# Down projection in another order, and its weight sums on VectorE: one core of a decoder layer

## The chip, the cores and the metric

The kernel runs on one NeuronCore of one Trainium2 chip. The metric is the time of one execution in microseconds (us) on the device. The kernel before takes 1776.47 us, the median of three runs.

## The reference

One decoder layer on a sequence of 256 positions, width 2048, all in float32: two parallel branches (a spatial gating unit and a gated delta rule), an output projection, a SwiGLU feed-forward network and a gated embedding. The change lies in the feed-forward network and in what follows it directly:

```python
D_FF = 5632
h = rms_norm(x, norm_ffn[i])
f_gate, f_up = jnp.split(h @ w_gate_up[i], 2, axis=-1)   # w_gate_up: 2048 x 11264
x = x + (jax.nn.silu(f_gate) * f_up) @ w_down[i]         # w_down: 5632 x 2048
ple_gate = jax.nn.sigmoid(rms_norm(x, ple_norm[i]) @ w_ple_gate[i])
```

## The kernel before, in words

**Halves.** All weights come from memory in tiles of 128 x 1024 float32 (512 KB), called halves and numbered in the order in which TensorE uses them. To get float32 accuracy from the faster matmul type, each half is split in two: ScalarE (ACT) rounds it into `whi` (`split_hi`, lines 423 and 433), VectorE (DVE) takes the rest, `wlo` (`split_lo`, line 447). TensorE (PE) multiplies `whi` by both parts of the other operand and `wlo` by its high part. There are four slots for raw weights and four for `whi` and `wlo` (`RING`), and the splits run three halves ahead (`LEAD`): at stage n of a phase ScalarE and VectorE first split half n+3 and then do whatever else the program puts at stage n. The high part of half n+3 can't be made before TensorE has finished half n-1, whose slot it takes. Every engine works its list strictly in order.

**Pairs and forms.** The gate-up and down projections go through "pairs": two blocks of 512 columns computed together, block 0 in the PSUM tile `acc[0]`, block 1 in `acc[1]`. A part of each pair is done by a seven-product scheme of the Strassen kind on 2 x 2 blocks (two tiles of positions, two blocks of columns, two halves of depth): a "unit". A unit reads four halves, B11, B12, B21, B22, into slots of their own (`unit[...]`), forms four sums of weights from them (T3 = B12 + B22, T1 = B12 + B11, T2 = T1 + B22, T4 = B21 + T2) and multiplies the seven matrices B11, T1, B21, B22, T3, T2, T4 with sums of the input (`sx`, made by `sum_inputs` and `sums_low` on VectorE and `sums_high` on ScalarE). T1 takes the slot of B12 and T4 that of B21. A form costs TensorE 6 matmuls of 128 x 512 (lines 1111 and 1114); a plain half costs 12 (lines 475 and 481). The products go to `ps[0]`, `ps[1]`, `acc[0]` (B21 and T4) and `acc[1]` (B22).

**Who makes the sums.** VectorE makes T3 and T2 (`sum_t3`, `sum_t2`, lines 2210 and 2220). T1 and T4 are made by transfers that add: GpSimd waits and issues `dma_start(..., accum_op=ALU.add)` of one SBUF tile onto another (lines 749 and 752), 16 units with two each.

**The order.** `PAIRS` writes the halves of each pair as a string: `f` is the next form of the current unit in the fixed order of `UNIT_FORMS`, `0` and `1` are plain halves of block 0 and block 1. The phases around the change run in this order: `ffn0` (plain), `ffn1` to `ffn5`, `down_a0`, `down_a1` (the down projection of the first 3072 features, two pairs of column blocks), `ffn6` to `ffn10`, `down_b0` and `down_b1` (the rest; `down_b1` is plain). An ffn pair has 19 halves and one unit, `down_a0` and `down_a1` 30 halves and two units each, `down_b0` 26 halves and two units. `SyncE` issues all loads in the order of use, each waiting until its slot is read.

**What happens at the ends of pairs.** When the last B11 of a pair is done, ScalarE copies `ps[0][:, 0]` (`copy_p1`); when T2 and T3 are done, VectorE combines `ps` (`lower_sums`, `upper_sums`, lines 2273 to 2283). TensorE's first form of the next pair, B11, waits for `upper_sums`, and for `ps_free`, which VectorE sets after `f_low` (lines 2169 and 2171), the low part of the transposed product of the last ffn pair. Its first plain half of block 0 waits for `acc_read[0]`, B22 for `acc_read[1]`. In an ffn pair these are given by `gate_add` (stage 13) and `up_add` (stage 0 of the next pair). In a down pair VectorE adds first the sums (`add_sums`, line 2304) and then the PSUM tile (`add_pair`, which is `add_block`, lines 2142 and 2144) to the residual `xtok`, in that order; line 2144 is the release of `acc_read`. These lie at stages 29 of one down pair and 0 and 1 of what comes next.

Of the kernel before, what the change touches and what calls it, by code (L numbers as in the profile page):

```python
# [23 lines left out]
ALU = mybir.AluOpType  # L24
# [49 lines left out]
UNIT_FORMS = (B11, T1, B21, B22, T3, T2, T4)  # L74
# [34 lines left out]
for _name, _order in PAIRS.items():  # L109
    _counts, PAIR_UNITS[_name] = {"0": 0, "1": 0}, []  # L110
    for _n, _c in enumerate(_order):
        _h = H0[_name] + _n
        if _c == "f":
            if not PLACE or len(PLACE[-1]) == len(UNIT_FORMS):
                PAIR_UNITS[_name].append(len(PLACE))
                PLACE.append({})
            _form = UNIT_FORMS[len(PLACE[-1])]
# [9 lines left out]
U_BASE, _u = {}, 0  # L127
for _name in PAIR_NAMES:
    U_BASE[_name] = _u
    _u += 4 if _name.startswith("ffn") else 6  # L130
# [41 lines left out]
def build(nc, win, wba, wa, wb, wo, wgu, wd, wpg, wpp, xT_d, xk_d, pT_d, cols_d, hv_d, gmw_d, gmb_d, fin_d, out_d):  # L172
# [180 lines left out]
    t1_added, t4_added, t_made, s_summed, s_split = (sem("t1_added"), sem("t4_added"), sem("t_made"), sem("s_summed"), sem("s_split"))  # L353
    p1_copied, u_made, sum_full = sem("p1_copied"), sem("u_made"), sem("sum_full")
# [193 lines left out]
    with nc.Block() as block:  # L548
# [78 lines left out]
        def _(pool):  # L627
# [142 lines left out]
        def _(pe):  # L770
# [366 lines left out]
            def pair(name, after={}, free_from=None):  # L1137

                for n in range(PER[name]):
                    h = H0[name] + n  # L1140
                    if h in PLAIN:
                        block, c = PLAIN[h]
                        if c == 0 and block == 0:
                            acc_free(pe, name, 0, 0, 0)
                        x = unit_of(name, 0)[0]
                        first = c == 0 and (True if block == 0 else (1,))
                        use_half(pe, name, 0, n, block, first, False, 2 * len(PAIR_UNITS[name]) + c, x, rows=True)
                    else:
# [28 lines left out]
            gemm("down_b1", 0, 0, 2 * PART_B, 0, 0, fx, rows=True, after={1: lambda: turn_x(1, 0), 4: lambda: turn_x(1, 1)})  # L1177
# [37 lines left out]
        def _(act):  # L1215
# [436 lines left out]
            def ffn(i, turned, extra={}):  # L1652
# [8 lines left out]
                             21: (copy_p1("down_a0", PART_A),)})  # L1661
            pair("down_a1", {17: (copy_p1("down_a1", PART_A),), 27: (sums_high(3, 0, PLACE[PAIR_UNITS["down_a1"][1]][T2]),)})
# [6 lines left out]
                             19: (copy_p1("down_b0", FB // 2),)})  # L1669
            for n in range(PER["down_b1"]):  # L1670
                split_hi(act, "down_b1", 0, n)
                if n == 2:
                    x_high(1, 0, C_PLE)
                if n == 5:
# [61 lines left out]
        def _(dve):  # L1736
# [486 lines left out]
            for n in range(2 * HWIDE):  # L2223
# [41 lines left out]
            def lower_sums(name, up, turned):  # L2265

                def stage():
# [3 lines left out]
                    dve.wait_ge(u_made, U_BASE[name])  # L2271
# [26 lines left out]

            def add_sums(name, half, sums, b):
# [20 lines left out]
            def ffn(i, before, turned, extra={}):  # L2320

                name, k = f"ffn{i}", PAIR_UNITS[f"ffn{i}"][0]
                stages = {0: before[0], 1: before[1], 11: (lower_sums(name, up_sum[i], i - 1),), 12: (upper_sums(name, up_sum[i]),),
                          13: (gate_add(i),), 14: (sum_t3(k + 1),), 15: (turned_low(i - 1),) if turned else (), 18: (sum_t2(k + 1),)}
# [4 lines left out]
            def finish_f(i):  # L2329
# [9 lines left out]
            pair("down_a0", {0: (up_add(5),), 1: (product(5),), 4: (turned_low(5),), 7: (sum_inputs(fx, 4, 2),), 9: (sums_low(2, 0),),  # L2339
                             11: (sum_t3(k + 1),), 17: (sum_t2(k + 1),), 25: (sum_t3(k + 2),),  # L2340
                             27: (lower_sums("down_a0", down_up, PART_A),), 28: (upper_sums("down_a0", down_up),),
                             29: (add_sums("down_a0", 0, gate_sum, 0), add_pair("down_a0", 0, 0, MB + 1), sum_t2(k + 2))})
            pair("down_a1", {0: (add_sums("down_a0", 1, down_up, 1),), 1: (add_pair("down_a0", 1, 1, MB + 2),),
                             7: (sum_t3(k + 3),), 13: (sum_t2(k + 3),), 21: (sum_t3(k + 4),),
                             25: (lower_sums("down_a1", down_up, PART_A), sum_inputs(ax, 0, 3)), 26: (upper_sums("down_a1", down_up),),
                             27: (add_sums("down_a1", 0, gate_sum, 2), sums_low(3, 0)),
                             28: (add_pair("down_a1", 0, 2, MB + 3), sum_t2(k + 4)), 29: (add_sums("down_a1", 1, down_up, 3),)})
            ffn(6, ((add_pair("down_a1", 1, 3, 2 * MB),), ()), False)
# [5 lines left out]
            pair("down_b0", {0: (up_add(10),), 1: (product(10),), 4: (turned_low(10),), 7: (sum_inputs(fx, 4, 5),), 9: (sums_low(5, 0),),  # L2354
                             10: (sum_t3(k + 1),), 15: (sum_t2(k + 1),),
                             24: (lower_sums("down_b0", down_up, FB // 2), upper_sums("down_b0", down_up)),
                             25: (add_sums("down_b0", 0, gate_sum, 0), add_pair("down_b0", 0, 0, 2 * MB + 1))})
            for n in range(PER["down_b1"]):
                split_lo(dve, "down_b1", 0, n)
                if n == 0:  # L2360
                    add_sums("down_b0", 1, down_up, 1)()
                    add_pair("down_b0", 1, 1, 2 * MB + 2)()
                if n == 2:
                    x_low(1, 0, C_PLE)
                if n == 5:
# [117 lines left out]
```

## Time and profile before

| | us |
|---|---|
| median of 3 runs | 1776.47 (1775.42 to 1777.78) |
| profiled execution | 1779.04 |
| its span | 1777.4 |
| PE busy | 1747.2 (98%) |
| DVE busy | 1268.2 (71%) |
| ACT busy | 922.7 (52%) |
| POOL busy | 256.7 (14%) |
| mean granted TensorE clock | 0.993 of 2.4 GHz |
| `unit<-unit` adding transfers | 32 of 512 KB, 6.2 to landing |

Busy time is the time in which an engine executed something. In a timeline the number before the engine is start and length; in square brackets stands how long the engine had been idle before and what released it. PE matmuls overlap each other a little, so the distance from start to start is the cost of one group, not the printed length.

### The profile page before, as it was taken

What the parts mean: (1) busy time and instruction counts of PE and PEld (TensorE: products, weight loads), DVE (VectorE), ACT (ScalarE), POOL (GpSimd) and SP (SyncE); (2) the same over time, 40 slices, a digit from 0 to 9 for tenths busy, and PEclk for the clock granted to TensorE, in tenths of its full rate; (3) what the DMA queues carried; (4) which work ended last, traced back from release to release, by engine and by line L of the source; (5) the groups of instructions that cost most, each with busy time, mean ns of one, the idle gap of its engine ahead of it and who ended that gap; (6) DMA issues with size and microseconds to landing.
All of it is one profiled execution on the core that took longest, in us unless ns stands there. A gap on an engine that the chain in (4) does not pass through costs nothing.

```text
span 1777.4 us, 24725 instructions
## 1 busy us (share of the span) xinstructions
PE 1747.2 (98%) x8888; PEld 1470.5 (83%) x8888; DVE 1268.2 (71%) x1496; ACT 922.7 (52%) x1019; POOL 256.7 (14%) x379
## 2 busy tenths in 40 slices
PE   9999999999999999999999999999999999998998
PEld 7888888889888888888888888887778888877887
DVE  7698887988867545455566778776777787767666
ACT  7764464555555444444445555545455555544455
POOL 5035070431610000000010000000000000001011
PEclk9999999999999999999999999999999999999999
DMA  8566465474657666666667776776777777755663
GB/s 272 173 187 189 145 204 167 141 218 135 193 167 227 190 194 191 192 189 189 189 196 219 217 225 211 236 212 197 207 223 229 231 215 225 211 163 166 191 210 133
DMA packets 108614, 349.59 MB, mean 197 GB/s; under 512 B 23712, under 2 KB 24112, under 8 KB 108272
## 3 DMA queue, kind: packets, MB, share of 16 engines
q1 hardware_dynamic: 88448, 320.12, 57.1%
q0 software_dynamic: 5696, 22.81, 6.7%
q10 hardware_dynamic: 14384, 5.52, 1.3%
q8 instruction: 54, 0.88, 0.2%
q14 instruction: 32, 0.26, 0.0%
HBM read 328.46 MB, written 3.16 MB: 187 GB/s over the span
## 4 chain that ended last, share of the span: by engine, by line
PE 83%; issue 5%; POOL 4%; DVE 3%; DMA 2%; ACT 2%; ACTq 0%; POOLq 0%; DVEq 0%; SPq 0%
PE acc L475 40%; PE acc L481 20%; PE acc L454 7%; PE acc L459 3%; PE ps L1111 3%; PE acc L1111 2%; POOL blk_t L676 2%; POOL blk_x L678 2%; PE ps L1114 1%; DVE wlo L447 1%; DMA unit<-unit 1%; PE acc L1114 1%; ACT whi L433 1%; PE ps L1085 1%; DMA diagT<-inv_out 0%
## 5 line engine op out<-in xcount | busy, mean ns | idle before, releaser
L447 DVE TENSOR_TENSOR wlo<-raw,whi 128x1024 fp32r<-128x1024 f32 x540 | 682.9, 1271 | 399.0 <-ACT whi L433 386.7
L433 ACT ACTIVATE whi<-raw 128x1024 fp32r<-128x1024 f32 x539 | 568.3, 1058 | 601.5 <-PE acc L481 468.2
L475 PE MATMUL acc<-whi,ax 128*128 128x512 f32 x2176 | 540.7, 390 | 1.6 <-DVEq L2144 1.4
L475 PEld LDWEIGHTS acc<-whi,ax 128*128 128x128 f32 x2176 | 406.2, 188 | 86.7 <-issue 1.8
L481 PE MATMUL acc<-wlo,ax 128*128 128x512 f32 x1088 | 291.1, 389 | 0.0
L481 PEld LDWEIGHTS acc<-wlo,ax 128*128 128x128 f32 x1088 | 204.2, 188 | 42.9 <-DVE wlo L447 0.3
L454 PE MATMUL acc<-ax,whi 128*128 128x512 f32 x896 | 228.6, 397 | 0.1
L454 PEld LDWEIGHTS acc<-ax,whi 128*128 128x128 f32 x896 | 160.9, 189 | 30.4 <-ACTq L1445 0.3
L447 DVE TENSOR_TENSOR wlo<-unit,whi 128x1024 fp32r<-128x1024 f32 x112 | 136.9, 1224 | 63.2 <-ACT whi L423 57.0
L423 ACT ACTIVATE whi<-unit 128x1024 fp32r<-128x1024 f32 x112 | 118.7, 1061 | 103.0 <-PE acc L481 56.5
L475 PE MATMUL acc<-whi,fx 128*128 128x512 f32 x512 | 133.0, 404 | 8.6 <-DVEq L2144 8.6
L459 PEld LDWEIGHTS acc<-ax,wlo 128*128 128x128 f32 x896 | 122.2, 190 | 9.0
L475 PEld LDWEIGHTS acc<-whi,fx 128*128 128x128 f32 x512 | 99.7, 196 | 30.5 <-DVEq L2144 9.4
L459 PE MATMUL acc<-ax,wlo 128*128 128x256 f32 x896 | 124.8, 282 | 0.0
L742 POOL TENSOR_TENSOR sqsum<-sqsum,t 128x512 f32<-128x512 f32 x16 | 27.6, 1725 | 462.4 <-ACT t L1577 461.8
L676 POOL TENSOR_TENSOR blk_t<-blk_m,blk_x 128x60 f32<-128x60 f32 (+24 forms) x124 | 67.4, 543 | 99.8 <-DMA blk_m<-inv_in 90.4
L481 PE MATMUL acc<-wlo,fx 128*128 128x512 f32 x256 | 69.2, 393 | 0.0
L678 POOL TENSOR_TENSOR blk_x<-blk_x,blk_t 128x60 f32<-128x60 f32 (+24 forms) x124 | 64.5, 521 | 9.7
L749 POOL DMA_DIRECT2D unit<-unit x16 | 14.0, 874 | 356.2 <-DVE unit L2210 356.2
L475 PE MATMUL acc<-whi,mx 128*128 128x512 f32 x256 | 63.6, 391 | 0.0
L475 PE MATMUL acc<-whi,yb 128*128 128x512 f32 x256 | 63.2, 389 | 0.0
L481 PEld LDWEIGHTS acc<-wlo,fx 128*128 128x128 f32 x256 | 48.9, 191 | 10.4
(331 smaller groups left out, 1784.4 us busy)
## 6 DMA issues: line engine op xcount, KB each, us to landing
raw<-in_win SPq DMA_DIRECT2D x223, 512.0 KB, 4.2
raw<-in_wgu SPq DMA_DIRECT2D x136, 512.0 KB, 4.4
raw<-in_wd SPq DMA_DIRECT2D x64, 512.0 KB, 4.4
unit<-in_wgu SPq DMA_DIRECT2D x40, 512.0 KB, 4.6
raw<-in_wb SPq DMA_DIRECT2D x32, 512.0 KB, 4.1
raw<-in_wo SPq DMA_DIRECT2D x32, 512.0 KB, 4.0
unit<-unit POOLq DMA_DIRECT2D x32, 512.0 KB, 6.2
raw<-in_wpg SPq DMA_DIRECT2D x32, 512.0 KB, 4.2
```

The source lines that it names most:

```text
L423: nc.scalar.activation(whi[:, s], unit[b][:], ACT.Copy).then_inc(hi_done, 1)
L433: nc.scalar.activation(whi[:, s], raw[:, src], ACT.Copy).then_inc(hi_done, 1)
L447: nc.vector.tensor_tensor(wlo[:, s], src, whi[:, s].bitcast(F32), ALU.subtract).then_inc(lo_done, 1)
L454: return nc.tensor.matmul(o, whi[:, s, kt, m * P:(m + 1) * P], x[:, k].rearrange("p q n -> p (q n)"), start=begin, stop=end, skip_group_ch ...
L459: return nc.tensor.matmul(o[:, 0:SEQ], wlo[:, s, kt, m * P:(m + 1) * P], x[:, k, 0], start=begin, stop=end, skip_group_check=True)
L475: nc.tensor.matmul(into[buf][:, m], x[:, WIDE_K * h + kt, q, m * P:(m + 1) * P], whi_w[:, s, kt], start=(m in first if isinstance(first, t ...
L481: mm = nc.tensor.matmul(into[buf][:, m], x[:, WIDE_K * h + kt, 0, m * P:(m + 1) * P], wlo_w[:, s, kt], start=False, stop=last and kt == WI ...
L676: chain(g.tensor_tensor(tmp, blk_m[:, j + 1:32, j:j + 1].to_broadcast([P, r, c]), blk_x[:, j:j + 1, 0:c].to_broadcast([P, r, c]), ALU.mult ...
L678: chain(g.tensor_tensor(blk_x[:, j + 1:32, 0:c], blk_x[:, j + 1:32, 0:c], tmp, ALU.add), v + 3 + 2 * j)
L742: g.tensor_tensor(sqsum[:], sqsum[:], piece(t[1], a), ALU.add).then_inc(res["added"], 1)
L1111: mm(out, x(q, kt), whi_w[:, s, kt], start=begin and kt == 0 and q == 0, stop=False, skip_group_check=True)
L1114: last = mm(out, x(0, kt), wlo_w[:, s, kt], start=False, stop=end and kt == WIDE_K - 1, skip_group_check=True)
```

## The change

The forms get letters of their own, so that the order string says which form comes where (`a` B11, `b` T1, `c` B21, `d` B22, `e` T3, `g` T2, `h` T4). The ffn pairs keep their order. The second part of each down pair is reordered; in its last unit T4 comes before T2 and T3, and in `down_b0` B21 comes before T1. T1 and T4 are made by VectorE (`sum_t1`, `sum_t4`), and the adding transfers and GpSimd's waits for them are gone. The release of `acc[0]` and `acc[1]` after down pairs becomes a stage of its own (`add_acc`), separate from `add_sums`. `turned_low` moves from stage 4 to stage 3 in `down_a0` and `down_b0`. `copy_p1` and `lower_sums` wait for a count of residual updates (`res["x"]`, `X_DONE`) instead of `u_made`. Two transposes of `down_b1` go one half later.

```diff
-UNIT_FORMS = (B11, T1, B21, B22, T3, T2, T4)
+FORM_OF = {"a": B11, "b": T1, "c": B21, "d": B22, "e": T3, "g": T2, "h": T4}
-FFN_ORDER = "f0f0f0f0f0ff0111111"
+FFN_ORDER = "a0b0c0d0e0gh0111111"
-         "down_a0": "0000f0f0f0f0f1f1f1f1ff1ff1ff11", "down_a1": "f0f0f0f0f0f0f0f0f1f1f1f1f1f111",
+         "down_a0": "0000a0b0c0d0eg1ha1b1cd1hg1e111", "down_a1": "a0b0c0d0e0g0h0a0b1c1d1h1g1e111",
-         "down_b0": "0000f0f0ff1f1f1ff1fff1fff1"}
+         "down_b0": "0000a0c0bd1h1egac1bd1h1ge1"}
...
+X_DONE = {name: MB * (1 + (name != "down_a0" and PAIR_NAMES.index(name) > PART_A - 1)) for name in PAIR_NAMES}
+X_DONE["down_a1"] = MB + 2
...
-            for k in range(N_UNITS):
-                pool.wait_ge(unit_in[B11], 16 * (k + 1))
-                pool.wait_ge(t_made, 2 * k + 1)
-                pool.dma_start(unit[T1][:], unit[B11][:], accum_op=ALU.add).then_inc(t1_added, 16)
-                pool.wait_ge(lo_done, PLACE[k][B21] + 1)
-                pool.wait_ge(t_made, 2 * k + 2)
-                pool.dma_start(unit[T4][:], unit[T2][:], accum_op=ALU.add).then_inc(t4_added, 16)
...
-            gemm("down_b1", 0, 0, 2 * PART_B, 0, 0, fx, rows=True, after={1: lambda: turn_x(1, 0), 4: lambda: turn_x(1, 1)})
+            gemm("down_b1", 0, 0, 2 * PART_B, 0, 0, fx, rows=True, after={2: lambda: turn_x(1, 0), 5: lambda: turn_x(1, 1)})
...
+            def sum_t1(k):
+                def stage():
+                    dve.wait_ge(unit_in[B11], 16 * (k + 1))
+                    dve.wait_ge(t_made, 2 * k + 1)
+                    v.tensor_tensor(unit[T1][:], unit[B12][:], unit[B11][:], ALU.add).then_inc(t1_made, 1)
+            def sum_t4(k):
+                def stage():
+                    dve.wait_ge(lo_done, PLACE[k][B21] + 1)
+                    dve.wait_ge(t_made, 2 * k + 2)
+                    v.tensor_tensor(unit[T4][:], unit[B21][:], unit[T2][:], ALU.add).then_inc(t4_made, 1)
...
+            def add_acc(name, half, b):
+                def stage():
+                    count = 2 * [x for x in PAIR_NAMES if x.startswith("down")].index(name) + half + 1
+                    dve.wait_ge(half_used, pair_end(name, half) + 1)
+                    x = xtok[:, :, WIDE * b:WIDE * (b + 1)]
+                    v.tensor_tensor(x, acc[half][:], x, ALU.add).then_inc(acc_added, 1)
+                    dve.wait_ge(acc_added, count)
+                    dve.sem_inc(acc_read[half], 1)
...
-                    dve.wait_ge(u_made, U_BASE[name] + 4 + half)
+                    dve.wait_ge(u_made, U_BASE[name] + (2, 4)[half])
-                    v.tensor_tensor(x, x, sums, ALU.add).then_inc(u_made, 1)
+                    v.tensor_tensor(x, x, sums, ALU.add).then_inc(res["x"], 1)
...
-          13: (gate_add(i),), 14: (sum_t3(k + 1),), 15: (turned_low(i - 1),) if turned else (), 18: (sum_t2(k + 1),)}
+          13: (gate_add(i),), 14: (sum_t3(k + 1),), 15: (turned_low(i - 1),) if turned else (), 16: (sum_t1(k + 1),), 18: (sum_t2(k + 1),)}
           (and 4: (sum_t4(k),) in the same dictionary)
...
+pair("down_a0", {0: (up_add(5),), 1: (product(5),), 3: (turned_low(5),), 6: (sum_t4(k),), 7: (sum_inputs(fx, 4, 2),), 9: (sums_low(2, 0),),
+                 11: (sum_t3(k + 1), sum_t1(k + 1)), 14: (sum_t2(k + 1),), 18: (sum_t4(k + 1),),
+                 24: (add_acc("down_a0", 0, 0), sum_t3(k + 2)), 26: (sum_t1(k + 2),), 27: (lower_sums("down_a0", down_up, PART_A),),
+                 28: (upper_sums("down_a0", down_up),), 29: (add_sums("down_a0", 0, gate_sum, 0),)})
+pair("down_a1", {0: (add_acc("down_a0", 1, 1),), 1: (sum_t2(k + 2),), 2: (sum_t4(k + 2),), 3: (add_sums("down_a0", 1, down_up, 1),),
+                 7: (sum_t3(k + 3),), 9: (sum_t1(k + 3),), 10: (sum_t2(k + 3),), 12: (sum_inputs(ax, 0, 3),), 17: (sum_t4(k + 3),),
+                 23: (add_acc("down_a1", 0, 2),), 24: (sum_t3(k + 4),), 26: (sum_t1(k + 4),), 27: (lower_sums("down_a1", down_up, PART_A),),
+                 28: (sums_low(3, 0), upper_sums("down_a1", down_up)), 29: (add_sums("down_a1", 0, gate_sum, 2),)})
+ffn(6, ((add_acc("down_a1", 1, 3),), (sum_t2(k + 4),)), False, {3: (add_sums("down_a1", 1, down_up, 3),)})
...
+pair("down_b0", {0: (up_add(10),), 1: (product(10),), 3: (turned_low(10),), 5: (sum_t4(k),), 7: (sum_inputs(fx, 4, 5),), 9: (sums_low(5, 0),),
+                 11: (sum_t3(k + 1), sum_t1(k + 1)), 13: (sum_t2(k + 1),), 16: (sum_t4(k + 1),),
+                 22: (add_acc("down_b0", 0, 0),), 25: (lower_sums("down_b0", down_up, FB // 2),)})
             for n in range(PER["down_b1"]):
                 split_lo(dve, "down_b1", 0, n)
                 if n == 0:
+                    upper_sums("down_b0", down_up)()
+                    add_sums("down_b0", 0, gate_sum, 0)()
+                if n == 1:
+                    add_acc("down_b0", 1, 1)()
                     add_sums("down_b0", 1, down_up, 1)()
```

## Rows read from the trace of the kernel before

**Rows 1.** Timeline of PE, end of `down_b0`, start of `down_b1` (start, us, instruction, count, [idle before]).
```profile
1598.49 1.07 PE L1111 MATMUL ps<-whi,sx 128*128 128x512 f32 x4
...
1603.03 1.07 PE L481 MATMUL acc<-wlo,fx 128*128 128x512 f32 x4
1608.93 3.78 PE L475 MATMUL acc<-whi,fx 128*128 128x512 f32 x8 [4.84 <-DVEq L2144]
...
1614.08 2.00 PE L475 MATMUL acc<-whi,fx 128*128 128x512 f32 x8
```
**Rows 2.** Timeline of PE, first form of `down_a0`.
```profile
1202.12 1.08 PE L481 MATMUL acc<-wlo,fx 128*128 128x512 f32 x4
1206.86 1.38 PE L1111 MATMUL ps<-whi,fx 128*128 128x512 f32 x4 [3.65 <-DVEq L2171]
...
1212.69 1.08 PE L1111 MATMUL ps<-whi,sx 128*128 128x512 f32 x4
```
**Rows 3.** Timeline of PE, first plain half of `down_a1`.
```profile
1261.20 0.61 PE L1114 MATMUL ps<-wlo,fx 128*128 128x512 f32 x2
1265.54 3.63 PE L475 MATMUL acc<-whi,fx 128*128 128x512 f32 x8 [3.72 <-DVEq L2144]
...
1269.98 1.09 PE L1111 MATMUL ps<-whi,sx 128*128 128x512 f32 x4
```
**Rows 4.** Timeline of PE, first plain half of `ffn6`.
```profile
1329.39 0.61 PE L1114 MATMUL ps<-wlo,ax 128*128 128x512 f32 x2
1331.38 2.11 PE L475 MATMUL acc<-whi,ax 128*128 128x512 f32 x8 [1.37 <-DVEq L2144]
...
1335.61 1.98 PE L475 MATMUL acc<-whi,ax 128*128 128x512 f32 x8
```
**Rows 5.** Timeline of PE, first form of `down_b0`.
```profile
1555.51 1.07 PE L481 MATMUL acc<-wlo,fx 128*128 128x512 f32 x4
1560.28 2.04 PE L1111 MATMUL ps<-whi,fx 128*128 128x512 f32 x4 [3.70 <-DVE fx L2169]
...
1567.19 1.09 PE L1111 MATMUL ps<-whi,sx 128*128 128x512 f32 x4
```
**Rows 6.** Windows after the gap in `ffn6`: length, busy of PE, PEld, DVE, ACT, POOL, granted clock, DMA.
```profile
1331.00:1333.00 2.00, 1.62 (x7) 1.37 (x8) 1.76 (x3) 0.16 (x1) 0.00 (x0) 1.00 0.59 231
```
**Rows 7.** Timeline of ACT at the start of `down_a0` and of `down_a1`.
```profile
1200.62 1.01 ACT L1594 ACTIVATE fx<-ps 128x1024 fp32r<-128x1024 f32 x1
...
1260.71 1.06 ACT L423 ACTIVATE whi<-unit 128x1024 fp32r<-128x1024 f32 x1 [4.54 <-DMA unit<-unit]
```
**Rows 8.** Timeline of DVE, end of `ffn5` and start of `down_a0`.
```profile
1187.14 1.23 DVE L447 TENSOR_TENSOR wlo<-raw,whi 128x1024 fp32r<-128x1024 f32 x1 [1.49 <-ACT whi L433]
...
1192.59 1.22 DVE L447 TENSOR_TENSOR wlo<-raw,whi 128x1024 fp32r<-128x1024 f32 x1 [0.36 <-ACT whi L433]
1193.73 1.22 DVE L2251 TENSOR_TENSOR t<-acc,t 128x1024 f32<-128x1024 f32 x1
...
1200.75 1.23 DVE L447 TENSOR_TENSOR wlo<-unit,whi 128x1024 fp32r<-128x1024 f32 x1 [1.50 <-ACT whi L423]
...
1205.53 1.22 DVE L2169 TENSOR_TENSOR fx<-ps,fx 128x1024 fp32r<-128x1024 f32 x1
```
**Rows 9.** All instructions on `unit` tiles: VectorE's T3 sums, and transfers.
```profile
L2210 DVE TENSOR_TENSOR unit<-unit,unit x16: 1214/1218/1220, 964.8 to 1578.7; 128x1024 f32<-128x1024 f32 x16
...
DMA to landing us min/median/max: 3.4/5.2/7.9
```
**Rows 10.** Timeline of DVE, start of `ffn6`: a sum behind an add whose end is waited for.
```profile
1331.51 1.23 DVE L2220 TENSOR_TENSOR unit<-unit,unit 128x1024 f32<-128x1024 f32 x1 [0.24 <-DVE xT L2142]
```
**Rows 11.** Timeline of DVE in `down_b0`: first operation of `sum_inputs`, and the split behind it.
```profile
1571.07 0.68 DVE L2182 TENSOR_TENSOR xhalf<-fx 128x512 f32<-128x512 f32 x1
...
1574.18 1.22 DVE L447 TENSOR_TENSOR wlo<-unit,whi 128x1024 fp32r<-128x1024 f32 x1
```
**Rows 12.** One window of the length of an ffn pair, with `sum_inputs` in it.
```profile
1098.00:1141.00 43.00, 43.00 (x195) 35.65 (x195) 36.53 (x39) 23.77 (x25) 1.74 (x2) 1.00 0.74 220
```

More of the change, by code:

```diff
@@ L112 @@
         _h = H0[_name] + _n
-        if _c == "f":
-            if not PLACE or len(PLACE[-1]) == len(UNIT_FORMS):
+        if _c in FORM_OF:
+            if not PLACE or len(PLACE[-1]) == len(FORM_OF):
                 PAIR_UNITS[_name].append(len(PLACE))
                 PLACE.append({})
-            _form = UNIT_FORMS[len(PLACE[-1])]
+            _form = FORM_OF[_c]
             PLACE[-1][_form] = _h
@@ L125 @@
 N_UNITS = len(PLACE)
[L127 to L130, printed above, removed]
+U_BASE = {name: 4 * j for j, name in enumerate(PAIR_NAMES)}
+X_DONE = {name: MB * (1 + (name != "down_a0" and PAIR_NAMES.index(name) > PART_A - 1)) for name in PAIR_NAMES}
+X_DONE["down_a1"] = MB + 2
 S_EVENT = {**{(f"ffn{i}", 0): 0 for i in range(1, PART_A)}, ("down_a0", 0): 1, ("down_a1", 0): 1, ("down_a0", 1): 2, ("down_a1", 1): 2,
@@ L1660, in _ @@
             pair("down_a0", {3: (turned_high(PART_A - 1),), 9: (sums_high(2, 0, PLACE[PAIR_UNITS["ffn5"][0]][T2]),),
-                             21: (copy_p1("down_a0", PART_A),)})
-            pair("down_a1", {17: (copy_p1("down_a1", PART_A),), 27: (sums_high(3, 0, PLACE[PAIR_UNITS["down_a1"][1]][T2]),)})
+                             19: (copy_p1("down_a0", PART_A),)})
+            pair("down_a1", {17: (copy_p1("down_a1", PART_A),), 27: (sums_high(3, 0, PLACE[PAIR_UNITS["down_a1"][1]][T3]),)})
             ffn(6, False)
@@ L1668, in _ @@
             pair("down_b0", {3: (turned_high(FB // 2 - 1),), 9: (sums_high(5, 0, PLACE[PAIR_UNITS["ffn10"][0]][T2]),),
-                             19: (copy_p1("down_b0", FB // 2),)})
+                             18: (copy_p1("down_b0", FB // 2),)})
             for n in range(PER["down_b1"]):
                 split_hi(act, "down_b1", 0, n)
-                if n == 2:
+                if n == 3:
                     x_high(1, 0, C_PLE)
-                if n == 5:
+                if n == 6:
                     x_high(1, 1, C_PLE)
@@ L2322, in ffn @@
                 name, k = f"ffn{i}", PAIR_UNITS[f"ffn{i}"][0]
-                stages = {0: before[0], 1: before[1], 11: (lower_sums(name, up_sum[i], i - 1),), 12: (upper_sums(name, up_sum[i]),),
-                          13: (gate_add(i),), 14: (sum_t3(k + 1),), 15: (turned_low(i - 1),) if turned else (), 18: (sum_t2(k + 1),)}
+                stages = {0: before[0], 1: before[1], 4: (sum_t4(k),), 11: (lower_sums(name, up_sum[i], i - 1),), 12: (upper_sums(name, up_sum[i]),),
+                          13: (gate_add(i),), 14: (sum_t3(k + 1),), 15: (turned_low(i - 1),) if turned else (), 16: (sum_t1(k + 1),), 18: (sum_t2(k + 1),)}
                 for n, more in extra.items():
@@ L2338, in _ @@
             k = PAIR_UNITS["down_a0"][0]
[L2339 to L2347, printed above, removed]
@@ L2353, in _ @@
             k = PAIR_UNITS["down_b0"][0]
[L2354 to L2357, printed above, removed]
+            pair("down_b0", {0: (up_add(10),), 1: (product(10),), 3: (turned_low(10),), 5: (sum_t4(k),), 7: (sum_inputs(fx, 4, 5),), 9: (sums_low(5, 0),),
+                             11: (sum_t3(k + 1), sum_t1(k + 1)), 13: (sum_t2(k + 1),), 16: (sum_t4(k + 1),),
+                             22: (add_acc("down_b0", 0, 0),), 25: (lower_sums("down_b0", down_up, FB // 2),)})
             for n in range(PER["down_b1"]):
```

36 lines of the change are left out of this document (16 added, 20 removed).

## The prediction

> **What bounds the kernel now.** I read the page's busy shares first: PE has 98% of the span, so the time is PE's work plus the gaps in it. Then the waits of PE over the stretch from `ffn1` to `down_b1`: five, all released by VectorE, and none anywhere else in that stretch. Then the timeline of PE around each, and of VectorE and ScalarE to see what the release waited for.
>
> A matmul costs 0.227 us from start to start: from 1598.49 to 1603.03 PE does two forms of 6 and the 8 high matmuls of a plain half, 20 in 4.54 [rows 1]. So a form is 1.36, a plain half 2.72, its last 4 matmuls 0.91, a form's last two 0.45. With these prices each gap's whole loss can be read, from the last undisturbed matmul to the first group back in step:
> - First form of `down_a0`: due at 1202.12 + 0.91 = 1203.03, starts at 1206.86 (3.83 late); the second form is due a form and a plain half later, at 1207.11, and starts at 1212.69. Loss 5.6 [rows 2].
> - First plain half of `down_a1`: due 1261.65, starts 1265.54 (3.9 late); the form after it due 1264.37, starts 1269.98. Loss 5.6 [rows 3].
> - First plain half of `ffn6`: due 1329.84, starts 1331.38 (1.5 late); the plain half after the next form due 1333.92, starts 1335.61. Loss 1.7 [rows 4].
> - First form of `down_b0`: due 1556.42, starts 1560.28 (3.9 late); the second form due 1560.50, starts 1567.19. Loss 6.7 [rows 5].
> - First half of `down_b1`: due 1603.94, starts 1608.93 (5.0 late); the second due 1606.66, starts 1614.08. Loss 7.4 [rows 1].
>
> Together 27.0: 18.1 is idle and 8.9 comes after the idle time, when matmuls take up to twice as long (8 in 3.78, later 8 in 2.00 [rows 1]), as at 1.2 instead of 2.4 GHz. After the shortest gap the granted clock stayed 1.00 [rows 6], and its surplus is only 0.15.
>
> **The change part by part.** Times below are counted from the start of a pair's first half on PE; in step, VectorE starts the split of stage n 1.36 after PE starts half n (1200.75 against a half that ends 2.72 before 1202.12 + 0.91, plus the transposes of 0.9 behind it: 1199.4 [rows 2, 8]). Back to back its operations on 1024 columns come every 1.14 [rows 8]. An add whose end the next one waits for takes 1.47: 1.22 and 0.25 [rows 10].
>
> *PE's work* is the same: 14, 14 and 14 forms and 16, 16 and 12 plain halves in the three down pairs, before and after.
>
> *`turned_low` one stage earlier (gaps 1 and 4).* Now `f_low` stands behind the split of stage 4, which can't begin before the plain half in front of the gap is finished: it runs 1205.53 to 1206.75, and PE starts 0.11 later. At stage 3 it follows the split that starts at 1200.75, so it starts at 1201.89; the high part it needs is done at 1201.63 [rows 7, 8]. It ends at 1203.11, and PE's form starts at 1203.22 instead of 1203.03: 0.2 remains in each. Gain 5.4 + 6.5 = 11.9.
>
> *`add_acc` before the sums (gaps 2, 3, 5).* In `down_a0` T4 ends at 50.1 now (half 23) and its release runs at stage 24, about 52.6 to 53.8, against a need at 65; in `down_a1` at about 50 against 64; in `down_b0` at 48.6 against 52.8. `acc[1]` is released at stage 0 or 1 of the next pair, at about 5, and is needed at 12 (B22), in `down_b1` at 27. What is late next is `upper_sums`, on which the next pair's first form waits. VectorE's list in `down_a0` from stage 24: split 51.4, release 52.6 to 54.05 with its wait, T3, split, split, T1 to 58.6, split, two lower sums to 61.1, split, two upper sums: the last ends at 63.5, and PE comes at 63.7. No gap, or a few tenths. In `down_a1` the sum on the inputs' low part stands there too (`sums_low`): the last upper sum ends at 62.7, PE comes at 62.56, gap 0.3. In `down_b0` they have moved into `down_b1`, whose first half doesn't need them. Also in `down_a1` ScalarE waited 4.5 for T1's adding transfer [rows 7]; a VectorE sum ends at 58.6, 2.6 ahead of the split of it. Gain 5.5 + 1.4 + 7.4 = 14.3.
>
> *T1 and T4 on VectorE.* 32 sums of 1.22, priced as T3's [rows 9], 39 in all, in place of 32 transfers. Beside PE they cost nothing if VectorE doesn't fall so far behind that PE waits for a `wlo`. How far may that be? In step, the split of half n+3 ends 2.6 after half n starts and is needed 1.8 into a plain half (0.9 into a form): a lag of over 5 us even where two forms stand between. In an ffn pair T1 (stage 16) and T4 (stage 4) fall where VectorE idles 1.49 per stage [rows 8] or catches up within three stages. The worst ffn pairs are `ffn3` and `ffn8`: T1, then the seven operations of `sum_inputs`, 3.1 [rows 11], make stage 16 5.4 long where 2.7 is to be had: lag 2.7, and with `up_add` and the product at most 2.9. `down_b0` is tighter: split 26 x 1.14, plus about 20 of the rest, 50 of 53; my list lags most (2.9) at stage 14 and always ends a `wlo` over 1 us before its use. Cost 0; the other bound is in the rivals.
>
> *New waits.* `copy_p1` of `ffn6` on ScalarE now waits for `add_sums` of the last block at VectorE's stage 3, about 10.6, instead of about 6. Behind it the high part of half 7 comes at 11.2 to 12.3, and PE needs it at 13.6: 1.3 to spare. SyncE is held at B12's load until T2 is made, at 7.0 in `down_a1` and `ffn6`; the plain loads behind it are for halves that start after 17, and loads take 3.4 to 7.9 [rows 9]. T3 of `down_a1`'s second unit may wait for its load a microsecond or two on VectorE, which has 5 to spare there. Cost 0, upper bound one gap as small as that of `ffn6`, 1.7 [rows 4].
>
> *Less DMA, no GpSimd work here, transposes of `down_b1` one half later:* 0, PE needs none of them sooner. I take no gain from the freed transfers, since no PE wait in this stretch ends on a load.
>
> Sum: 11.9 + 14.3 = 26.2 of the profiled 1779.04, to 1752.8. The median of before is 2.6 below that execution; the same saving on it gives 1776.5 - 26.2 = 1750.3, which I forecast.
>
> A doubt on the residual gaps: after an idle of 1.4 the clock stayed at 2.4 GHz [rows 6], so 0.2 to 0.3 should cost themselves only. The Trainium skill (TensorE: Matmul & The Clock Gate, section "Part 1: The HAM clock gate") says that "the default state is throttled, and activity releases the throttle". Read strictly, four small gaps would each bring the slow stretch back, 4 x 1.8, and the time would be 1757.5; that row speaks against it.
>
> **The rivals.**
> 1. *`upper_sums` or ScalarE's new wait takes the gap's place.* Margins of -0.3 to +0.2 at two places and 1.3 at a third are smaller than a few slips of VectorE. For it: these places are serial lists of 8 to 10 operations. Against: the sums repeat within 0.01 [rows 9]. A gap of 1.5 to 4 at one to three of them costs 1.7 to 5.6 each [rows 3, 4]: 5 to 11 more, 1755 to 1761. In it I count the small gaps with a slow clock (4 x 1.8, 1757.5).
> 2. *A unit's load comes late.* B21 of `down_b0`'s second unit is loaded after T4's split (24.2) and ScalarE wants it at 30; the longest landing is 7.9 [rows 9]. Then PE waits at the third or fourth form after; 2 to 5, 1752 to 1755.
> 3. *Slower: VectorE becomes the bound in the ffn pairs.* In a window of 43.0 with `sum_inputs` it is busy 36.5 [rows 12]; two sums more make 38.9. If sums of two SBUF tiles were slowed by loads or the lag passed 5 us before a pair's first forms, each of ten pairs would get a gap of 1.5 and half of them a slow stretch of 1.8 or more: 24 to 33, plus 5 from the tight ends: against 26 gained, 1779 to 1788. It decides from 4 us more VectorE work a pair than I count. Against: T3 and T2 took 1.22 every time, in full traffic.
> 4. *Nothing gained:* the gaps are there for a second reason right behind (1.9 of 3.8 left each). Each releaser's list was followed above; I see none.
>
> **How the numbers follow.** Forecast (1747.5 to 1754): 0.72; rival 1: 0.15; rival 2: 0.06; rival 3: 0.04; rival 4: 0.03. The range that holds 8 of 10: 1747.5 to 1758. Down from the forecast lie the 0.8 of small gaps not coming, and the runs' spread of about 1.3. A run can tell apart some 0.2% (3.6 us), so faster 0.95, same 0.02, slower 0.03.
>
> **What would show it.** PE's waits on VectorE between `ffn1` and `down_b1` fall from 17.3 (the sum of the five brackets in [rows 1 to 5]) to under 1.5, and the granted clock of the ten microseconds from the start of `down_b0`'s first form is 1.00. VectorE is 37 to 39 busier; `f_low` runs right behind the split of half 6. Rival 1 would show a PE wait at the first form of `down_a1` or `ffn6`, released by line 2283's successor, or at half 7 of `ffn6` by ScalarE; rival 2 a wait of ScalarE on a load of `unit`; rival 3 PE waits on `wlo` in every ffn pair. The prediction is wrong if PE's gaps are gone and the time still falls by less than 22, or if a gap of over 1 us stands in the ffn pairs.

## The result and the profile after

The changed kernel takes 1752.15 us, the median of four runs (1751.16 to 1752.55), against 1777.12 of the kernel before in the same round: a ratio of 0.9859, 95% interval 0.9842 to 0.9876, so 25.0 us less (22 to 28). The profiled execution takes 1751.86, 27.2 less than that of before.

The busy shares of the changed kernel; those of before are in the table ahead of the prediction.
```profile
PE 1737.8 (99%) x8888; PEld 1464.4 (84%) x8888; DVE 1300.6 (74%) x1528; ACT 921.3 (53%) x1019; POOL 232.2 (13%) x347
```
PE does the same 8888 matmuls in 9.4 us less busy time; 8.9 of it is what the prediction read as slow matmuls behind the gaps.

The timeline of PE in the changed kernel at the five places, in the order of [rows 2], [rows 3], [rows 4], [rows 5] and [rows 1]; the last row is the first matmul after `down_b1`.
```profile
1200.97 1.08 PE L481 MATMUL acc<-wlo,fx 128*128 128x512 f32 x4
1202.07 1.20 PE L1104 MATMUL ps<-whi,fx 128*128 128x512 f32 x4
...
1206.28 1.07 PE L1104 MATMUL ps<-whi,sx 128*128 128x512 f32 x4
...
1254.81 0.63 PE L1107 MATMUL ps<-wlo,fx 128*128 128x512 f32 x2
1255.27 1.98 PE L475 MATMUL acc<-whi,fx 128*128 128x512 f32 x8
...
1315.56 1.07 PE L481 MATMUL acc<-wlo,fx 128*128 128x512 f32 x4
1316.69 1.15 PE L1104 MATMUL ps<-whi,ax 128*128 128x512 f32 x4
...
1542.12 1.07 PE L481 MATMUL acc<-wlo,fx 128*128 128x512 f32 x4
1543.28 1.16 PE L1104 MATMUL ps<-whi,fx 128*128 128x512 f32 x4
...
1583.28 1.07 PE L481 MATMUL acc<-wlo,fx 128*128 128x512 f32 x4
1584.18 1.98 PE L475 MATMUL acc<-whi,fx 128*128 128x512 f32 x8
...
1641.28 1.98 PE L475 MATMUL acc<-whi,px 128*128 128x512 f32 x8
```
With the prices of the prediction (0.91 after an L481 group) what is left is 1202.07 - 1201.88 = 0.19 at `down_a0`, nothing at `down_a1`, 1316.69 - 1316.47 = 0.22 at `ffn6`, 0.25 at `down_b0` and nothing at `down_b1`: 0.7 of 27.0.

From the low part in front of the first gap to the first matmul behind `down_b1` the changed kernel takes 1641.28 - 1200.97 = 440.31; before, 1668.48 - 1202.12 = 466.36. That is 26.05 less. The other 1.15 of the profiled difference is there before `ffn1`, the first pair that the change touches: its first form starts at 975.86 before and at 974.71 now. It belongs to the two executions, not to the change.

The timeline of VectorE in the changed kernel: the split and `f_low` at `down_a0` (of before in [rows 8]), and the last upper sum of `down_a0` and of `down_a1`.
```profile
1199.60 1.23 DVE L447 TENSOR_TENSOR wlo<-unit,whi 128x1024 fp32r<-128x1024 f32 x1 [1.50 <-ACT whi L423]
1200.74 1.22 DVE L2160 TENSOR_TENSOR fx<-ps,fx 128x1024 fp32r<-128x1024 f32 x1
...
1252.99 0.68 DVE L2292 TENSOR_TENSOR t<-ps,t 128x512 f32<-128x512 f32 x1
...
1315.91 0.68 DVE L2292 TENSOR_TENSOR t<-ps,t 128x512 f32<-128x512 f32 x1
```
`f_low` now follows the split by 1.14. The last upper sum of `down_a0` ends at 1253.67, 0.2 before PE's first form of `down_a1` at 1253.89, which is on time. That of `down_a1` ends at 1316.59, 0.1 before PE starts `ffn6` at 1316.69: PE waited for it, and this is the 0.22.

ScalarE's new wait, in the timeline of ScalarE at stage 3 of `ffn6`:
```profile
1327.16 0.60 ACT L1624 ACTIVATE t<-ps 128x512 f32<-128x512 f32 x1 [3.62 <-DVE xT L2324]
1327.65 1.05 ACT L433 ACTIVATE whi<-raw 128x1024 fp32r<-128x1024 f32 x1
```
It waited 3.6, and the high part behind it ended at 1328.70, 1.7 before PE used it at 1330.38. The window that answers to [rows 12], and the `unit` view that answers to [rows 9]:
```profile
1097.00:1140.00 43.00, 43.00 (x196) 35.65 (x195) 38.30 (x41) 23.32 (x25) 0.00 (x0) 1.00 0.62 197
```
```profile
L2217 DVE TENSOR_TENSOR unit<-unit,unit x16: 1217/1218/1222, 985.4 to 1569.4; 128x1024 f32<-128x1024 f32 x16
...
DMA to landing us min/median/max: 3.3/4.3/7.8
```
VectorE is at 38.3 of 43.0 where it was at 36.5, with PE busy throughout. The median landing of 4.3 instead of 5.2 does not compare like with like, since the 5.2 has the adding transfers in it; the loads of `unit` from `in_wgu` alone went from 4.6 to 4.1.

### The profile page after: what moved, and what is told of

Its sections match the earlier page's. It is cut to its first block, busy times and chain, and to the rows that moved or that the text cites. A ratio compares the mean times of both kernels' runs of the same rounds, so it can differ in the third digit from the quotient of the medians.

```text
span 1750.2 us, 24721 instructions
## 1 busy us (share of the span) xinstructions
PE 1737.8 (99%) x8888; PEld 1464.4 (84%) x8888; DVE 1300.6 (74%) x1528; ACT 921.3 (53%) x1019; POOL 232.2 (13%) x347
## 4 chain that ended last, share of the span: by engine, by line
PE 82%; issue 7%; POOL 6%; DVE 2%; ACT 2%; ACTq 0%; POOLq 0%; DMA 0%; DVEq 0%; SPq 0%
PE acc L475 41%; PE acc L481 20%; PE acc L454 4%; PE ps L1104 3%; POOL blk_t L676 3%; POOL blk_x L678 3%; PE acc L1104 2%; PE acc L459 2%; PE ps L1107 2%; PE acc L1107 1%; DVE wlo L447 1%; ACT whi L433 1%; PE ps L1078 1%; DVE conv_k L1795 0%; PE acc L1090 0%
## 5 line engine op out<-in xcount | busy, mean ns | idle before, releaser
L481 PE MATMUL acc<-wlo,ax 128*128 128x512 f32 x1088 | 291.1, 389 | 0.1
L481 PEld LDWEIGHTS acc<-wlo,ax 128*128 128x128 f32 x1088 | 204.2, 188 | 43.0 <-DVE wlo L447 0.5
L475 PE MATMUL acc<-whi,fx 128*128 128x512 f32 x512 | 127.0, 390 | 0.0
L475 PEld LDWEIGHTS acc<-whi,fx 128*128 128x128 f32 x512 | 95.8, 188 | 19.7
L481 PE MATMUL acc<-wlo,fx 128*128 128x512 f32 x256 | 68.4, 389 | 0.0
L481 PEld LDWEIGHTS acc<-wlo,fx 128*128 128x128 f32 x256 | 48.1, 188 | 10.0
```

The lines of the kernel that those rows point to most:

```text
L475: nc.tensor.matmul(into[buf][:, m], x[:, WIDE_K * h + kt, q, m * P:(m + 1) * P], whi_w[:, s, kt], start=(m in first if isinstance(first, t ...
L481: mm = nc.tensor.matmul(into[buf][:, m], x[:, WIDE_K * h + kt, 0, m * P:(m + 1) * P], wlo_w[:, s, kt], start=False, stop=last and kt == WI ...
```

## The experiments

Ratios are to the kernel before, run on the same chip in turn. "More" is counted from the changed kernel's ratio, times 1777. The intervals of two such ratios leave about 4 us of doubt on their difference, so differences of 1 to 4 us are not shown by the ratios alone. They rest on two things more: no execution of the runs concerned is as fast as the slowest of the changed kernel (1752.55), and each trace shows the waits themselves. The last column has the time in the trace from the first form of `ffn1` to the first matmul behind `down_b1`, for one execution each; in the kernel before it is 692.62.

| run | us | ratio (95%) | PE waits in the stretch | stretch (to changed) |
|---|---|---|---|---|
| changed | 1752.15 | 0.9859 (0.9842 to 0.9876) | none listed; 0.7 by the starts | 666.57 |
| `u_turn4` | 1764.03 | 0.9918 (0.9893 to 0.9944) | 3.7 + 3.7 | 679.11 (+12.5) |
| `u_release` | 1755.89 | 0.9877 (0.9857 to 0.9897) | 1.1 + 1.9 | 670.17 (+3.6) |
| `u_b1c` | 1757.72 | 0.9885 (0.9868 to 0.9901) | 3.7 | 672.21 (+5.6) |
| `u_pool` | 1762.4 | 0.9914 (0.9891 to 0.9936) | 1.6 + 3.4 + 0.3 | 676.44 (+9.9) |
| `p_t1c` | 1754.72 | 0.9870 (0.9854 to 0.9887) | 0.7 + 1.0 + 0.3 | 669.88 (+3.3) |
| `p_t4c` | 1755.0 | 0.9874 (0.9858 to 0.9891) | 0.3 + 1.3 | 669.13 (+2.6) |
| `b_turn3` | 1767.33 | 0.9947 (0.9928 to 0.9966) | 4.6 + 1.4 + 4.8 | 681.25 (11.4 under before) |
| `b_dve` | 1774.87 | 0.9985 (0.9976 to 0.9995) | the five places, 15.3; 0.3 elsewhere | 690.75 (1.9 under before) |
| `d2` | 1753.78 | 0.9866 (0.9850 to 0.9883) | 1.0 | 668.53 (+2.0) |
| `d4` | 1772.72 | 0.9975 (0.9964 to 0.9985) | 12.6 | 688.01 (+21.4) |

**The gaps, one place at a time.** `u_turn4`:
```diff
-3: (turned_low(5),), 6: (sum_t4(k),)      # down_a0
+4: (turned_low(5),), 6: (sum_t4(k),)
-3: (turned_low(10),), 5: (sum_t4(k),)     # down_b0
+4: (turned_low(10),), 5: (sum_t4(k),)
```


> The changed kernel with turned_low (the low part of the last transposed product, which frees ps[0]) put back from stage 3 to stage 4 in down_a0 and down_b0. Theory of the gaps: the two gaps before the first form of down_a0 and down_b0 come back in full, each 3.8 to 3.9 us of waiting and 1.8 to 2.9 of slow matmuls behind it, in place of 0.2: 11.9 more, 1764. The other three places stay without a gap. Rival (adding transfers: the gaps at these places came partly from their traffic): less than 8 more.

Timeline of PE in that run, at both places:
```profile
1200.45 1.08 PE L481 MATMUL acc<-wlo,fx 128*128 128x512 f32 x4
1205.19 2.08 PE L1104 MATMUL ps<-whi,fx 128*128 128x512 f32 x4 [3.66 <-DVEq L2162]
...
1211.79 1.07 PE L1104 MATMUL ps<-whi,sx 128*128 128x512 f32 x4
...
1552.41 2.04 PE L1104 MATMUL ps<-whi,fx 128*128 128x512 f32 x4 [3.70 <-DVE fx L2160]
```
Both gaps are back at their old length, and the one in `down_a0` costs 6.4 in all (the second form due 1205.43, starts 1211.79). 10.5 more by the ratios, 11.9 by the medians, as expected. The adding transfers had no part in these two gaps: they are absent here, and the gaps are back.

The same edit alone, on the kernel before, is `b_turn3`:
```diff
-4: (turned_low(5),)   -4: (turned_low(10),)
+3: (turned_low(5),)   +3: (turned_low(10),)
```


> The kernel before with one edit: turned_low at stage 3 instead of 4 in down_a0 and down_b0. Theory: the gaps at the first form of down_a0 and of down_b0 shrink to 0.2, the three others stay as they are: 11.9 less, 1765. Rival (what is late next takes the gap's place, since the order and the transfers are the old ones): under 8 less.

9.4 less by its ratio (6 to 13), 9.9 by the medians of its round (1777.22 and 1767.33), where 11.9 was expected; both gaps are gone. The one in `down_a1` grew, as PE's timeline shows:
```profile
1260.83 3.48 PE L475 MATMUL acc<-whi,fx 128*128 128x512 f32 x8 [4.60 <-DVEq L2144]
```
4.6 instead of 3.7 [rows 3]: PE came earlier, the release did not keep step. So the rival was right at one place, for 0.9.

`u_release` puts two releases back behind the sums:
```diff
-24: (add_acc("down_a0", 0, 0), sum_t3(k + 2))      ... 29: (add_sums("down_a0", 0, gate_sum, 0),)
+24: (sum_t3(k + 2),)      ... 29: (add_sums("down_a0", 0, gate_sum, 0), add_late("down_a0", 0, 0, MB + 1))
-23: (add_acc("down_a1", 0, 2),)   ... 29: (add_sums("down_a1", 0, gate_sum, 2),)
+29: (add_sums("down_a1", 0, gate_sum, 2), add_late("down_a1", 0, 2, MB + 3))   # half 1 likewise, at stages 0 and 1
```
`add_late` waits for the sum on the same block of `xtok` and then runs `add_acc`.

> The changed kernel with the release of the accumulators of down_a0 and down_a1 put back behind add_sums: add_sums and then the accumulator's add at stage 29, 0 and 1, as in the kernel before; order of halves and sums on VectorE as changed, down_b0 untouched. Theory: PE waits at its first plain half of block 0 in down_a1 (release at about 67.1 from the start of down_a0, due 65.0: a gap of 2.1) and in ffn6 (2.4), so 4.5 of waiting and up to 1.8 each of slow matmuls: 5 to 8 more, 1757 to 1760. These are gaps of a length between the 1.5 that left the clock alone and the 3.8 that didn't. Rival (the order of the forms, T4 before T2 and T3, closed those gaps by itself): under 1 more.

Timeline of PE, and one window behind the longer gap (granted clock third from the end):
```profile
1256.05 2.12 PE L475 MATMUL acc<-whi,fx 128*128 128x512 f32 x8 [1.10 <-DVEq L2316]
...
1321.16 2.12 PE L475 MATMUL acc<-whi,ax 128*128 128x512 f32 x8 [1.91 <-DVEq L2316]
```
```profile
1321.00:1323.00 2.00, 1.84 (x8) 1.53 (x9) 1.85 (x3) 0.00 (x0) 0.00 (x0) 1.00 0.00 0
```
Both gaps are back, each shorter than expected by 0.5 to 1.0 (VectorE was a little earlier than my list), and without slow matmuls: 3.2 to 3.7 more, under the 5 to 8 expected, so this expectation was missed. The rival (under 1 more) is out.

`u_b1c` moves the third release only. This is not quite its old place: in the kernel before it stood behind the upper sums and `add_sums` at stage 25 of `down_b0`; here it stands one stage later and in front of them.
```diff
-22: (add_acc("down_b0", 0, 0),), 25:
+25:
 if n == 0:
+    add_acc("down_b0", 0, 0)()
     upper_sums("down_b0", down_up)()
```


> The changed kernel with one release moved back: the add of acc[0] of down_b0 (add_acc) from stage 22 of down_b0 to stage 0 of down_b1, in front of the upper sums. Theory of the gaps: the release comes at about 56.7 from the start of down_b0, PE's first half of down_b1 is due at 52.8: a gap of 3.9, and 1.8 to 2.9 of slow matmuls behind it: 5.7 to 6.8 more, 1758 to 1759. It is the third of the three places of the release, of which the run that put back two others showed 3.7. Rival (the reordered tail of down_b0, not the early release, closed the gap): under 1 more.

PE's timeline there:
```profile
1583.61 1.07 PE L481 MATMUL acc<-wlo,fx 128*128 128x512 f32 x4
1588.34 2.72 PE L475 MATMUL acc<-whi,fx 128*128 128x512 f32 x8 [3.66 <-DVEq L2316]
...
1595.57 1.98 PE L475 MATMUL acc<-whi,fx 128*128 128x512 f32 x8
```
The third half, at 1595.57, was due at 1584.52 + 5.44 = 1589.96: 5.6, as the medians say (4.6 by the ratios). The expected 5.7 to 6.8 is just missed, with a gap of 3.7 for 3.9. The rival is out.

**The sums' place.** `u_pool` gives T1 and T4 back to GpSimd's adding transfers; `p_t1c` only T1, `p_t4c` only T4.
```diff
+            for k in range(N_UNITS):
+                pool.wait_ge(unit_in[B11], 16 * (k + 1))
+                pool.wait_ge(t_made, 2 * k + 1)
+                pool.dma_start(unit[T1][:], unit[B11][:], accum_op=ALU.add).then_inc(t1_made, 16)
+                ...
# sum_t1 and sum_t4 do nothing; waits count in steps of 16
```


> The changed kernel with T1 and T4 made by GpSimd's adding transfers again, everything else as changed. Theory that the sums on VectorE only make the new order possible: no change in the ffn pairs; in down_a0's second unit T4 lands about 1 us late for PE, in down_b0's second unit T1 lands at about 36.7 and holds VectorE's T2, so the low part of half 17 is 2.2 late; in all 3 to 6 us of PE waiting, 1755 to 1760. Rival 1 (the sums' place is indifferent, only the release order and turned_low count): within 1 of the changed kernel, 1751 to 1753. Rival 2 (the transfers took bandwidth or ports from the loads or from VectorE all along): over 8 more.

PE waited for T4 in `down_a0`, as expected (1.6 for about 1), but hardly in `down_b0` (0.3 for 2.2), and most in `down_a1`, where I had expected nothing. Timelines of PE and of VectorE, and the `unit` view:
```profile
1242.00 1.20 PE L1111 MATMUL acc<-whi,fx 128*128 128x512 f32 x4 [1.62 <-ACT whi L423]
...
1290.69 1.22 PE L1114 MATMUL ps<-wlo,fx 128*128 128x512 f32 x2 [3.44 <-DVE wlo L447]
```
```profile
1278.54 1.23 DVE L2208 TENSOR_TENSOR unit<-unit,unit 128x1024 f32<-128x1024 f32 x1 [4.76 <-DMA unit<-in_wd]
...
1288.27 1.23 DVE L2230 TENSOR_TENSOR unit<-unit,unit 128x1024 f32<-128x1024 f32 x1 [5.09 <-DMA unit<-unit]
```
```profile
DMA to landing us min/median/max: 3.3/5.2/10.4
```
In `down_a1` VectorE's T3 waited 4.8 for a load and T2 then 5.1 for T1's transfer, which can't start before T3. All splits queue behind these two, so PE ran out of a low part, and slow matmuls followed. 9.8 to 10.2 more, not 3 to 6. That is the number of rival 2 (over 8), but not its "all along": 20 of the 32 transfers belong to the units of the ffn pairs, and PE showed no wait there, while `b_dve` below, which takes the transfers away from the kernel before, gains only about 3. The two halves of it:

> The changed kernel with T1 alone made by the adding transfer, T4 by VectorE. The run with both by transfers was 10 slower and showed PE waits of 1.6 in down_a0 (T4 landed late) and 3.4 in down_a1 with slow matmuls behind it: there T3 waited 4.8 for a load that took 10.4, and T2 then 5.1 for T1's transfer. Theory (the long wait needs both: T4's transfer among the loads makes the load late, T1's transfer then adds its own latency): neither wait appears, 0.4 at down_b0 as in that run: 0 to 1.5 more, 1752 to 1754. Rival (T1's transfer is enough, since VectorE's T2 stands behind it in order): the wait in down_a1 stays, over 5 more.

> The changed kernel with T4 alone made by the adding transfer, T1 by VectorE. Theory: the wait of 1.6 for T4 in down_a0 stays and costs about 2; the load of B22 in down_a1 is late again (over 8 instead of under 7) and T3 waits for it, but T1 and T2 follow at once on VectorE, so PE waits under 1 there: 2 to 3.5 more, 1754 to 1756. Rival (the late load by itself is what held PE): 3 or more of waiting in down_a1, over 6 more. Rival (loads are late whatever the transfers do, it was chance): T3 doesn't wait for a load here.

```profile
1229.40 1.17 PE L1108 MATMUL ps<-whi,sx 128*128 128x512 f32 x4 [0.65 <-ACT whi L423]
...
1289.47 0.74 PE L1111 MATMUL ps<-wlo,sx 128*128 128x512 f32 x2 [0.99 <-DVE wlo L447]
```
These are PE's waits with T1 alone. With T4 alone the view of VectorE's waits has
```profile
DVE unit L2205 <- DMA unit<-in_wd: 3.2, 1, 3.2
```
and PE's timeline at the first form of `down_a1`
```profile
1256.26 1.17 PE L1108 MATMUL ps<-whi,fx 128*128 128x512 f32 x4 [1.04 <-issue]
```
The view of transfers has the load of B22 in `down_a1`, in the changed kernel (issued at 1264.15) and in `u_pool` (issued at 1268.11):
```profile
unit<-in_wd SPq DMA_DIRECT2D x1, 512.0 KB, 5.8
...
unit<-in_wd SPq DMA_DIRECT2D x1, 512.0 KB, 10.3
```
The same load lands in 5.7 with T1's transfers alone and in 10.2 with T4's alone, whose transfer is issued among the same loads and takes 10.5 itself. With T4's transfer the loads around it also go out closer together, by 1.1 to 1.2 us, which is less than the 4.4 to 4.5 that this load is later. So the load is late because of T4's transfer, and not by chance.

T1 alone costs 2.0 to 2.6 (3.3 in the stretch), where 0 to 1.5 was expected; T4 alone 2.7 to 2.9, inside its 2 to 3.5; together they cost 10, not 5 to 6. The long wait is made of a load late beside T4's transfer and T1's transfer behind it. With T4 alone the load is late again and holds VectorE for 3.2, but PE doesn't wait there, so the late load alone is not enough. The 1.6 for T4 itself shrank to 0.3, so most of it came from T1's transfer, which held T2. In its place PE lost 1.0 at the first form of `down_a1` and 0.3 at that of `ffn6`: each starts 0.1 behind the end of VectorE's last upper sum (1256.16 and 1319.31), the tight ends of rival 1. With T1 alone VectorE waited for T1's transfer three times, at most 4.6, and PE 1.0 in `down_a1`: the theory that neither wait appears was wrong there.

`b_dve` makes the sums on VectorE in the kernel before, everything else as it was (`sum_t1` and `sum_t4` at stages 16 and 4 of the ffn pairs, 13, 20 and 26 and so on in the down pairs).

> The kernel before with T1 and T4 made by VectorE, at the changed kernel's stages in the ffn pairs and at fitting stages in the down pairs; order of the halves, releases and turned_low as before. Theory: the gap in down_a1 falls from 3.9 to 1.7 to 2.5, since the split there waited for T1's transfer; the other four gaps stay within 0.5 (that of down_b1 from 5.0 to 4.7 or so); nothing new in the ffn pairs: 2 to 4 less, 1772 to 1775. Rival (the transfers' traffic was a cost of its own): over 8 less. Rival (VectorE becomes the bound): more than before.

2.7 less by the ratio (0.9 to 4.3), 3.1 by the medians, 1.9 in the stretch; both rivals are out. PE's wait in `down_a1`:
```profile
1262.77 2.11 PE L475 MATMUL acc<-whi,fx 128*128 128x512 f32 x8 [1.91 <-DVEq L2137]
```
1.9 instead of 3.7, the other four near what they were (3.7, 1.4, 3.7, and 4.6 for 4.8).

**How much VectorE may lag.** In the changed kernel, N = 2 or 4 more sums at the end of each of the ten ffn pairs:
```diff
-                    v.tensor_tensor(unit[T2][:], unit[T1][:], unit[B22][:], ALU.add).then_inc(t_made, 1)
+                    for _ in range(extra):        # 2 or 4
+                        v.tensor_tensor(unit[T2][:], unit[T1][:], unit[B22][:], ALU.add).then_inc(more_sums, 1)
+                        again[0] += 1
+                        dve.wait_ge(more_sums, again[0])
+                    v.tensor_tensor(unit[T2][:], unit[T1][:], unit[B22][:], ALU.add).then_inc(t_made, 1)
```


> The changed kernel with two more sums like T2 (same operands, each waited for, 1.47 us each, 2.9 in all) at stage 18 of each of the ten ffn pairs: 29 us more on VectorE. Theory of the cover: VectorE may lag some 4.7 us at stage 2 before PE waits for a low part. In eight pairs the lag reaches 3.3: nothing. Behind ffn3 and ffn8, which already lag 2.9 (sum_inputs), it reaches 5.8: one wait of about 1.1 each. In all 2 more, 1754. Rival (what counts is VectorE's mean load, which stays under PE's): 0 more. Rival (VectorE's delay is handed on to PE by the adds and the product at once): 15 or more.

> As the run with two more sums, but four at stage 18 of each ffn pair, 5.9 us. Theory of the cover: lag 6.2 at stage 2 of six ordinary pairs, so PE waits 1.5 in each; 4 us and some slow matmuls behind ffn3 and ffn8; at down_a0 and down_b0 the low part of the product comes 2.4 late, two gaps of 2.5. In all 20 to 32 more, 1772 to 1784. Rival (mean load): VectorE would be busy 44.8 in a 43 us window only in the two pairs with sum_inputs and less in the others, so under 6 more.

PE's waits with two more:
```profile
PE acc L1107 <- DVE wlo L447: 0.6, 2, 0.3
PE ps L1078 <- DVE t L2276: 0.4, 2, 0.2
```
and with four more, from PE's timeline (an ordinary pair, the pair behind `ffn3`, `down_a0`, the pair behind `ffn8`), and two windows:
```profile
1028.25 0.73 PE L1107 MATMUL acc<-wlo,ax 128*128 128x512 f32 x2 [0.40 <-DVE wlo L447]
...
1116.25 2.02 PE L481 MATMUL acc<-wlo,ax 128*128 128x512 f32 x4 [2.17 <-DVE wlo L447]
...
1208.94 1.97 PE L1078 MATMUL ps<-cols,t 128*128 128x128 f32 x8 [2.73 <-DVE t L2276]
...
1468.53 1.21 PE L481 MATMUL acc<-wlo,ax 128*128 128x512 f32 x4 [2.16 <-DVE wlo L447]
```
```profile
1118.00:1120.00 2.00, 2.00 (x6) 1.53 (x5) 2.00 (x4) 0.00 (x0) 0.00 (x0) 0.56 1.04 397
...
1468.50:1470.50 2.00, 1.97 (x8) 1.42 (x8) 1.85 (x2) 0.00 (x0) 0.00 (x0) 1.00 0.76 293
```
29 us more on VectorE cost 1.2 to 1.6, where 2 was expected; another 30 cost 19 more, in all 20.6, at the low end of the 20 to 32 expected. The waits with two more are at the pairs behind `ffn3` and `ffn8`, and at the transposes of `down_a0` and `down_b0`. So 2.9 more a pair is nearly free and 5.9 is not: of the second 30 us about two thirds reach PE. The limit lies between, and my estimate of it, a lag of 4 to 5 us at the start of a pair, fits both runs. A rule by mean load (under 6 more) is out.

## Why the prediction was right

- *The gaps were the whole gain.* 27.0 by the losses read off PE's timeline, 26.2 forecast after what stays, 26.05 measured between the two marks. The remaining 0.3 between 26.05 and 27.0 - 0.7 I have not located. The total does not depend on which part of the change closes which gap, and that split was partly wrong, as follows.
- *`turned_low`:* 11.9 forecast for the two places; 10.5 to 11.9 when undone, 9.4 to 9.9 when done alone (11.4 in the stretch, with 0.9 lost to the longer gap in `down_a1`). Residuals 0.19 and 0.25 against 0.2.
- *Releases:* 14.3 forecast for three places. Undoing two cost 3.2 to 3.7 and moving the third 4.6 to 5.6, together 8 to 9, with waits of 1.1, 1.9 and 3.7 in place of 3.7, 1.4 and 4.8. So the 14.3 are not the releases' alone. Part of the rest belongs to the sums on VectorE, which by themselves cut the wait in `down_a1` from 3.7 to 1.9 (`b_dve`). That the new order of the halves has the remainder is an inference: no run has the new order alone, and none the early releases alone.
- *Sums on VectorE at no cost:* right by the traces, in which no PE wait in the ffn pairs appears; 38.3 busy in the window against 38.9 worked out. VectorE's total rose by 32, not 37 to 39; that bound was too high, probably because instructions in a row overlap by about 0.08 each (1.22 long, 1.14 apart) and many that stood alone now stand in a row. But I took them as neutral ("Cost 0"), and counted a gain of theirs only in `down_a1`. They were what the new order rests on: without them 10 are lost. The expectation that this would cost 3 to 6 missed the load of B22 in `down_a1`, which I had noted as a wait of "a microsecond or two on VectorE"; with transfers beside it it became 4.8.
- *Tight ends:* for the upper sums 0.2 to spare was forecast in `down_a0` and a gap of 0.3 behind `down_a1`; measured are 0.2 to spare and a gap of 0.22. ScalarE's margin was 1.3 by the forecast, 1.7 measured. These margins held, but `p_t4c` shows how little it takes: there the same two places cost 1.0 and 0.3.
- *Small gaps and the clock:* three gaps of 0.19 to 0.25 (the fourth didn't come) left the granted clock at 1.00 in the microseconds behind them, so the strict reading of the Trainium skill's "the default state is throttled" (TensorE: Matmul & The Clock Gate, "Part 1: The HAM clock gate") did not apply to them.
- *Rival 3* ("It decides from 4 us more VectorE work a pair"): at 2.9 more, 1.2 to 1.6 lost; at 5.9 more, 20.6. That fits, though nothing between the two was run. In an ordinary pair the loss at 5.9 was about 1.0 (PE's half at 1031.75, due 1030.77), not 1.5.

The forecast of 1750.3 is 1.85 under the measured median. Of this 0.65 is that the kernel before has a median of 1777.12 in this round, not 1776.47, and 1.2 that the saving by medians is 25.0, not 26.2 (26.05 in the profiled stretch). The spread of the runs of before (1775.4 to 1778.5) is larger than both, so that the forecast came within 2 us is partly luck.

## What to carry to other kernels

When one engine is busy 98% of the span, list its few waits, and price each from the last undisturbed instruction to the first one back in step: here a third of the loss came after the wait, as slow matmuls. Then move the release first: an instruction that frees a buffer belongs ahead of those that merely must be done (`b_turn3`, one such move, gave 9 to 11 of the 25). An engine with a queue of prepared tiles ahead of its consumer has a lag budget; count it where the consumer's steps are shortest, and fill it up to that, leaving a margin for a late load.

## What the hardware showed that I had not expected

The slow matmuls behind a gap do not follow from its length alone. In these traces 1.9 left the granted clock at 1.00, 2.17 brought 0.56 at one place and 2.16 left 1.00 at another; all 15 gaps of 2.7 and more brought slow matmuls, worth 1.5 to 3.0 us. The same gap of 3.65 to 3.66 at the first form of `down_a0` cost 5.6 in all in the kernel before, 6.4 in `u_turn4` and 6.7 in `b_dve`. What decides between them no run here shows. And a 512 KB adding transfer from SBUF to SBUF issued among five loads took 10.4 us to land, where the median of the 32 in that run is 6.7; a load issued beside it took 10.3, where it takes 5.8 without it, and held VectorE for 4.8.
